# One inference step of a two-layer hybrid decoder: all pages of the key/value cache issued from GpSimd's queue instead of from two queues in turn

## The reference

```python
past_k = cache_k[j, page_table].reshape(nb, -1, DA_HEADS, 2 * DA_DIM)
past_v = cache_v[j, page_table].reshape(nb, -1, DA_HEADS, 2 * DA_DIM)
...
keys = jnp.concatenate([past_k.astype(k_rows.dtype), k_rows], axis=1).reshape(b, p + s, DA_HEADS, 2, DA_DIM)
vals = jnp.concatenate([past_v.astype(v_rows.dtype), v_rows], axis=1)
mask = jnp.arange(p + s)[None, :] <= (p + jnp.arange(s))[:, None]
attn = diff_attend(q, keys, vals, mask, lam)
```

## Time and profile before

| | us |
|---|---|
| median of 3 runs | 2992.75 |
| lowest and highest | 2990.01, 2995.84 |
| the profiled execution, its own time | 2990.32 |
| its span, first to last instruction | 2988.7 |
| TensorE (PE) busy | 2803.8 (94%) |
| VectorE (DVE) busy | 1042.8 (35%) |
| ScalarE (ACT) busy | 831.8 (28%) |
| GpSimd (POOL) busy | 279.3 (9%) |
| DMA, mean over the span | 75 GB/s |
| key pages, issue to landing, SyncE and GpSimd (median) | 4.1, 4.5 |
| value pages, issue to landing, SyncE and GpSimd (median) | 5.2, 5.8 |

### The profile page before, as it was taken

One profiled execution on the slowest core, in us unless ns is written; L12 is line 12 of the kernel. 1 busy time (PEld: TensorE's weight loads), 2 busy tenths in 40 slices (PEclk: granted clock), 3 DMA queues, 4 the chain that ended last, 5 costly groups with the idle time before them and its releaser, 6 DMA issues.

```text
span 2988.7 us, 46335 instructions
## 1 busy us (share of the span) xinstructions
PE 2803.8 (94%) x19359; PEld 1857.4 (62%) x19359; DVE 1042.8 (35%) x1743; ACT 831.8 (28%) x1523; POOL 279.3 (9%) x317
## 2 busy tenths in 40 slices
PE   5999899997899999999879999999959999999997
PEld 4666565564566666666546666667636666666665
DVE  4455533324422102222372334343472221122224
ACT  4444322222322212221133332324332221122212
POOL 3000022212100000001110011010140000000010
PEclk8999999998999999999899999999979999999998
DMA  5211269730111211111244333321301112111211
GB/s 190 69 52 45 92 229 325 243 125 21 43 50 53 59 39 50 50 58 49 15 86 61 54 68 67 56 73 41 138 7 56 46 54 59 36 50 50 61 40 58
DMA packets 250826, 225.51 MB, mean 75 GB/s; under 512 B 10308, under 2 KB 217466, under 8 KB 250108
## 3 DMA queue, kind: packets, MB, share of 16 engines
q1 hardware_dynamic: 232764, 149.46, 19.6%
q0 software_dynamic: 17856, 73.10, 6.8%
HBM read 195.70 MB, written 26.81 MB: 74 GB/s over the span
## 4 chain that ended last, share of the span: by engine, by line
PE 87%; DVE 6%; ACT 2%; issue 1%; POOL 1%; DMA 1%; SPq 1%; DVEq 0%; ACTq 0%; POOLq 0%; PEldq 0%
PE ps L248 71%; PE ps L1158 2%; DVE arena L522 2%; PE ps L1146 1%; PE ps L844 1%; PE ps L1721 1%; PE ps L1712 1%; PE ps L923 1%; PE ps L1690 1%; POOL arena L335 1%; DMA hT<-in_cache_v 1%; PE ps L1665 1%; PE ps L1704 1%; PE ps L1197 1%; DVE arena L445 1%
## 5 line engine op out<-in xcount | busy, mean ns | idle before, releaser
L248 PE MATMUL ps<-u,w_split 128*128 128x352 f16 (+1 forms) x10440 | 1608.1, 314 | 55.7 <-DVE u L471 37.8
L248 PEld LDWEIGHTS ps<-u,w_split 128*128 128x128 f16 (+1 forms) x10440 | 1017.5, 98 | 608.5 <-DVE u L471 43.4
L248 PE MATMUL ps<-arena,w_split 128*128 128x352 f16 x4320 | 651.9, 313 | 0.0
L248 PEld LDWEIGHTS ps<-arena,w_split 128*128 128x128 f16 x4320 | 422.2, 98 | 223.8 <-issue 3.2
L231 DVE SCALAR_TENSOR_TENSOR w_split<-w_raw,w_split 128x1024 f16<-128x1024 f32 (+2 forms) x194 | 269.3, 1388 | 816.4 <-ACT w_split L218 816.3
L218 ACT ACTIVATE w_split<-w_raw 128x1024 f16<-128x1024 f32 (+2 forms) x194 | 211.7, 1091 | 78.4 <-PE ps L248 76.4
L578 ACT ACTIVATE arena<-arena 128x352 f16<-128x352 f32 x132 | 65.6, 497 | 390.1 <-DVE arena L610 390.1
L610 DVE SCALAR_TENSOR_TENSOR arena<-ps,arena 128x352 f32<-128x352 f32 x132 | 69.2, 524 | 287.2 <-PE ps L248 287.2
L572 ACT ACTIVATE arena<-ps 128x352 f32<-128x352 f32 x132 | 61.0, 465 | 329.1 <-PE ps L248 329.1
L332 POOL COPY arena<-arena 128x1056 f32<-128x1056 f32 x4 | 4.3, 1064 | 1227.5 <-ACT arena L591 1203.3
L335 POOL TENSOR_TENSOR arena<-arena 128x1056 f32<-128x1056 f32 x28 | 68.5, 2448 | 236.1 <-ACT arena L591 175.6
(11 more groups left out here) (339 smaller groups left out, 2083.2 us busy)
## 6 DMA issues: line engine op xcount, KB each, us to landing
w_raw<-in_w_gu SPq DMA_DIRECT2D x88, 512.0 KB, 3.8
w_raw<-in_w_in SPq DMA_DIRECT2D x56, 512.0 KB, 7.2
w_raw<-in_w_down SPq DMA_DIRECT2D x32, 704.0 KB, 4.6
hT<-in_cache_k SPq DMA_DIRECT2D x64, 256.0 KB, 4.1
hT<-in_cache_k POOLq DMA_DIRECT2D x64, 256.0 KB, 4.5
hT<-in_cache_v SPq DMA_DIRECT2D x64, 256.0 KB, 5.2
hT<-in_cache_v POOLq DMA_DIRECT2D x64, 256.0 KB, 5.8
h_spill<-hT POOLq DMA_DIRECT2D x2, 4224.0 KB, 13.3
```

The source lines that it names most:

```text
L248: ins = pe.matmul(ps[0:m, bank, 0:GW], w_split[:, v % 2, wp, k * w + col * P:k * w + col * P + m], x[:, xp, k0 + k, cols(g)], start=(k == ...
```

## The change

`load_page` stays as it is. GpSimd's two loops lose their condition and issue every page in its order of use: 16 ahead, 240 in the stage. SyncE issues no page, `sp_samples` and `sp_proj0` are gone, and so are SyncE's three waits ahead of its first page; its panels follow one another in one loop, each with its own wait for `w_ready`. No other engine's program changes, nor do the ring, the semaphores or the order of use. Behind the diff's last hunk line numbers are 37 less than before.

```diff
--- before.py
+++ after.py
@@ -1092,34 +1092,6 @@
                 eng.wait_ge(page_used, f - RING + 1)
             eng.dma_start(ring[:, f % RING, :], cache[0, ds(page, 1), :, :, :].rearrange("a t h e -> (a t) (h e)")
                          ).then_inc(page_loaded[f % RING // 2], 16)
-
-        def sp_samples(sp):
-            f = RING
-            for _ in range(3):
-                yield
-            for _ in range(2):
-                for _ in range(32):
-                    if f // 2 % 2 == 0 and f < 2 * NB * NPG:
-                        load_page(sp, f)
-                        load_page(sp, f + 1)
-                    f += 2
-                    yield
-                for _ in range(4):
-                    yield
-                for _ in range(32):
-                    if f // 2 % 2 == 0 and f < 2 * NB * NPG:
-                        load_page(sp, f)
-                        load_page(sp, f + 1)
-                    f += 2
-                    yield
-                for _ in range(3):
-                    yield
-
-        def sp_proj0(sp, v0, v1_):
-            for v in range(v0, v1_ + 1):
-                load_tile(sp, v + 2)
-                for _ in range(6):
-                    yield
 
         def pe_samples(pe):
 
@@ -1997,16 +1969,9 @@
 
             for v in range(5):
                 load_tile(sp, v)
-            sp.wait_ge(ids_loaded, 16)
-            sp.wait_ge(x_spilled, 16)
-            sp.wait_ge(t_ready, KD)
-            for f in range(RING):
-                if f // 2 % 2 == 0:
-                    load_page(sp, f)
             for v in range(5, CXB + 5):
                 load_tile(sp, v)
-            woven(sp_samples(sp), sp_proj0(sp, CXB + 3, WO0 - 1), SAMPLE_FILL)
-            for v in range(WO0 + 2, END):
+            for v in range(CXB + 5, END):
                 load_tile(sp, v)
 
             for tt in range(NTT):
@@ -2058,8 +2023,7 @@
             pool.wait_ge(x_spilled, 16)
             pool.wait_ge(t_ready, KD)
             for f in range(RING):
-                if f // 2 % 2:
-                    load_page(pool, f)
+                load_page(pool, f)
 
             for h in range(HEADS):
                 for ev, src, dst, n in ((v_ev, v_nat, v_p, 2), (k_ev, k_nat, k_p, 2)):
```

## The result

| | us |
|---|---|
| before, median of 4 runs | 2993.97 (2990.01 to 2995.84) |
| with the change, median of 4 runs | 3042.64 (3042.27 to 3049.07) |
| ratio, 95% interval | 1.0169, 1.0152 to 1.0187 |
| with the change, the profiled execution and its span | 3042.95, 3041.3 |

What follows compares the result with a forecast made beforehand. GpSimd's issue, 1.173 us a page, was taken as the new bound: +3.3, +23.4 and +13.6 make +40.3 us, plus 2 for the clock, on 2990.32 gives 3032.6; with 2.4 to the median, forecast 3034, range 3020 to 3057.

Steps and rivals of the forecast that it cites:

- The likeliest case: In the page-load stage GpSimd's issue becomes the bound; chance 0.84, with its own ends at 3022 and 3058 us.
- the first fill: First 16 pages: eight more on GpSimd take 9.2 us, covered by a later store's 10.64 us wait; cost nothing.
- the panels: SyncE's weight panels, no longer behind page waits, could start earlier; claimed to be worth nothing.
- The step: GpSimd's queue in the stage: each page issue takes 1.173 us, counting number load, wait and DMA.
- The first issue of a stretch: Start of a V stretch: the first page's use, behind which the issues follow, put at 0.5 us.
- The start of V: V of round 0 and K of round 1 taken as one run of issues, 111 steps, +23.4 us.
- Landing: Time from a page's issue until TensorE can use it: 4.1 us, with 2.8 and 6.1 as ends.
- The clock: TensorE's clock lowered by waits in V, slowing the dependent work behind each V: 2 us, between 0 and 10.
- the end of the stage: Restore of the hidden state behind the last page moves with the stage, as does its reader; cost nothing.
- Transfers set the pace: Rival: transfers, not issue, pace the V stretches, so the kernel is not slower, about 2976 to 2990 us; chance 7%.
- The break-even: V stretches: above a GpSimd issue step of 0.88 us a page the kernel becomes slower.
- GpSimd waits for something that shows only when it is alone: Rival: GpSimd's full queue waits, for example for descriptor room; step 1.3 us adds some 25 us, 3059; chance 5%.

Runs made afterwards that it cites:

- experiment 1: Kernel with the change, but page numbers come from the program instead of the table, so other pages are read; 2987.32 us.
- experiment 2: Kernel with the change, but the number of each page is loaded and checked twice; 3155.21 us.
- experiment 6: Kernel with the change, but one load fetches the numbers of eight pages, same pages read; 3004.12 us.
- Experiment 7: Kernel with the change, but in V the half panel comes after the third pair of each three instead of after the first; 3043.62 us.
- experiment 5: Kernel with the change, but SyncE still waits at the same page counts as before ahead of its panels, without issuing pages; 3044.88 us.
- experiment 4: Kernel before, two queues, but SyncE issues one pair of pages of four and GpSimd three of four; 3001.93 us.
- the quarter split with eight numbers: Kernel before, but SyncE issues one pair of four, GpSimd three, and one load fetches eight page numbers; 2993.11 us.

## Why the prediction was right, point by point

The forecast was 3034 in a range of 3020 to 3057, slower with 0.93; measured are 3042.64. The likeliest case is the one that came true: GpSimd's issue became the bound, K was hit less than V, GpSimd caught up only in the softmax, and the first fill and the panels cost nothing. Experiments 1, 2 and 6 show the mechanism from both sides (step 0.54, 0.95, 1.21 and 1.75 us; 2987, 3004, 3043 and 3155 us).

That the time came out only 8.6 us above the forecast is in part luck. The stage was missed by 15.4 us, +55.7 against +40.3. The 2 us for the clock stood outside that sum, the rest of the kernel happened to be 2.8 us shorter, and the last 2 us lie in how the profiled executions stand to the medians. The last step of the sum has a slip besides: 3032.6 + 2.4 is 3035, not 3034. Of the signs that were named, V of 66.4 and 64.0 us was to be near 61, and the DMA share of 0.72 to 0.75 was to be 0.6 to 0.7.

- **The step** was priced at 1.173 us and is 1.206 to 1.218. This is the largest error: 47 x 0.033 + 111 x 0.038 + 47 x 0.045 = 7.9 of the 15.4 us. The common step was read correctly (1.168); the longer ones behind every 14th and 21st page were too few in the 32 steps that I averaged. The trace of before showed them: in the row of 458.15 to 464.28 five steps gave 1.226, which I kept for the high end. That same row follows a wait of 4.70 us for TensorE, so "in V it does not wait" held for the two rows of steps and not for the whole of V.
- **The first issue of a stretch** was put 0.5 us behind the first use. It is 1.38 us (432.85 to 434.23, 598.52 to 599.90) and 0.7 later than assumed in K: 2.5 us together.
- **The start of V** of round 0 was taken as one run of issues. TensorE uses one pair there, then a half panel that waits 2.43 us for VectorE and runs 3.44 us instead of 1.95, and the ring is full; so GpSimd stands from 435.39 to 440.36, 3.8 us more than its step. In this stretch, where the issue sets the pace, nothing makes that up. Experiment 7 removes it and shortens V by 3.7 us.
- **Landing** was 3.2 us instead of 4.1, the value that I chose between 2.8 and 6.1; but a last pair of keys takes 2.6 us from its landing to the end of its scores, not 1.6: between its transposes and its scores stand those of the pair before, 0.64 us, and a pause of 0.26. TensorE took as long for these steps before the change (403.99 to 406.55). In V of round 1 the last page landed at 660.29, while a half panel ran until 661.63. Together all this is +0.8 us. The Trainium skill's fit (DMA: Bandwidth & Descriptors, "Anatomy of one DMA") gave 2.6 us; the trace of the change, at 213 to 224 GB/s, comes to 3.2 in the median and 2.8 at best, nearer to it than to my 4.1.
- **The clock** was given 2 us, for the dependent work behind V. It fell in V, to 0.82 and 0.86 on average, as foreseen, but what stands behind V took the same time as before (7.1 us to K, 9.7 us to the projection): 0 there. It cost something where nothing was put, inside V, in half panels at which TensorE and not the next page was late (columns of the earlier trace rows):

```profile
435.90:439.40 3.50, 3.50 (x19) 1.71 (x23) 0.53 (x1) 0.39 (x1) 0.03 (x1) 0.56 0.34 116
```

  The first half panel ran at a granted clock of 0.56 in 3.44 us instead of 1.95, which is 1.5 of the 3.8 us above; the same half panel, behind the same wait, ran in 1.95 us in the kernel before and in experiments 2 and 6. The last one of round 1 took 3.06 us, 1.1 more than at full speed, and ended only behind the last page's landing. So the size of 2 us was about right, and its place was not.
- **Nothing for the panels, the first fill and the end of the stage**: right for the panels by experiment 5; the store behind the first fill and the parts around the stage show no shift.
- **The rivals.** "Transfers set the pace" fell: the DMA share went down to 0.72 to 0.75 and the time up. The break-even was put at 0.88 us a page; measured, steps of 0.91 and 0.95 (experiments 4 and 6) give 9 and 12 us more than before, and 0.71 (the quarter split with eight numbers) none. The rule of the Trainium skill that it rested on (DMA: Bandwidth & Descriptors, "Issuing engines are not separate DMA queues", that the sequencer's time is usually small relative to the DMA) does not hold for these pages: 1.21 us to issue against 0.81 us to move at the 323 GB/s of the earlier trace rows. The argument that I held against this rival from SyncE was right in its direction and wrong in its number (1.04 instead of 1.14).
- "GpSimd waits for something that shows only when it is alone" has a grain of truth in the longer step behind every 14th DMA, 0.43 / 14 = 0.03 us a page, but nothing like 0.13.

## What to carry to other kernels

Price a queue by its whole sequence per DMA (number load, checks, address work, wait, DMA instruction), take that step as a mean over a stretch long enough to hold its rare longer steps, and compare it with the consumer's pace in each stage separately: two queues that each look half idle may be just enough. When a queue turns from follower to bound, a stop of the consumer while the ring is full is added to the stage, though it was free before. If all transfers must go to one queue, make a page cheap first: numbers fetched eight at a time gave 38 of 49 us back.

## What the runs showed of the hardware that I had not expected

- Two kinds of longer step on GpSimd's queue. One is +0.43 us behind every 14th page DMA in the kernels where GpSimd issues all 240 pages of the stage (the change, experiments 2 and 6). Where it issues 180 of them (experiment 4) it is +0.52 us behind every 18th, so it isn't set by the queue's own count of DMAs alone. The other is some +0.3 us and comes after some 126 to 135 instructions of the queue, whether a page has 5, 6 or 9 of them. What causes them stays open.
- A load and check of a page number costs GpSimd's queue 0.54 us (1.17 to 1.71). Without number and address work a page DMA of 256 KB goes out every 0.54 us. SyncE's step with a number is 1.15 us in the mean, almost as long as GpSimd's.
- One software queue alone moved 302 GB/s in V of experiment 1, beside the weight panels; with them that is 325 GB/s, as much as the two queues together moved before (323).
